# Hymba layer: sums of squares from the columns of x, with DVE additions and PE, and a new order of the first loads and index transposes

## The reference

```python
def rms_norm(x, g):
    xf = x.astype(jnp.float32)
    y = xf * lax.rsqrt(jnp.mean(xf * xf, axis=-1, keepdims=True) + EPS)
    return (y * g.astype(jnp.float32)).astype(x.dtype)

def reference(x, norm_gain, w_in, w_out, final_gain):
    B, S, _ = x.shape                       # 1, 512, 1024
    ...
        u = rms_norm(h, norm_gain[layer])   # DEPTH = 1
        z = jnp.einsum('bsd,de->bse', u, w_in[layer])
        (q_a, k_a, v_a, g_a, q_i, k_i, w_i, q_r, k_r, v_r, g_r) = jnp.split(z, split_points, axis=-1)
        ...
        y_a = dsa_attention(q_a, k_a, v_a, q_i, k_i, w_i, topk).reshape(B, S, ATT_WIDTH)
        y_a = y_a * jax.nn.silu(g_a)
        ...
        y_r = retention(q_r, k_r, v_r).reshape(B, S, RET_V_WIDTH)
        y_r = y_r * jax.nn.silu(g_r)
        mix = jnp.concatenate([y_a, y_r], axis=-1)
        h = h + jnp.einsum('bse,ed->bsd', mix, w_out[layer])
    return rms_norm(h, final_gain)
```

## Time and profile before

| | |
|---|---|
| Time, median of 3 runs | 295.29 us (295.18 to 295.79) |
| The profiled execution | 295.84 us, its span 293.7 us |
| Granted clock of PE, mean of the span | 0.989 |
| Busy: PE, DVE, ACT, POOL | 281.2, 201.4, 143.1, 68.6 us |
| Moved by DMA | 30.09 MB |

### The profile page before, as it was taken

The page is one execution under the profiler, slowest core; times in us unless marked ns, Lnnn a source line. Parts: engine busy times, 40 slices in busy tenths (PEclk is TensorE's granted clock), DMA queues, the critical chain, the costliest instruction groups (busy, mean ns, idle before and its releaser), DMA issues.

```text
span 293.7 us, 4386 instructions
## 1 busy us (share of the span) xinstructions
PE 281.2 (96%) x1504; PEld 240.7 (82%) x1504; DVE 201.4 (69%) x410; ACT 143.1 (49%) x305; POOL 68.6 (23%) x121
## 2 busy tenths in 40 slices
PE   5998999999999999997999999999999999999991
PEld 5996888888878888886888888788888988888891
DVE  1865799999999997759984863629646634854341
ACT  4766946333544533571666444564534662350231
POOL 1027322335200049990400203022010020000211
PEclk9799999999999999999999999999999999999998
DMA  7997520422332072040404220130210407311123
GB/s 227 405 342 280 169 76 0 143 73 74 98 116 75 0 208 78 2 143 1 135 11 143 72 73 0 33 112 7 77 63 0 137 8 230 129 36 36 74 86 128
DMA packets 15092, 30.09 MB, mean 102 GB/s; under 512 B 1376, under 2 KB 2912, under 8 KB 15072
## 3 DMA queue, kind: packets, MB, share of 16 engines
q1 hardware_dynamic: 14064, 28.71, 30.3%
q10 hardware_dynamic: 1008, 1.12, 1.1%
HBM read 27.73 MB, written 2.10 MB: 102 GB/s over the span
## 4 chain that ended last, share of the span: by engine, by line
PE 75%; DVE 12%; DMA 5%; issue 3%; POOL 2%; ACT 1%; ACTq 0%; SPq 0%; POOLq 0%; DVEq 0%
PE bank L417 19%; PE bank L419 18%; PE bank L418 18%; PE bank L467 6%; DVE keys L1035 3%; PE bank L481 3%; DVE top L1033 3%; DMA x_h<-in_x 3%; DVE w_lo L947 2%; DMA w_raw<-in_w_in 2%; PE bank L495 2%; PE bank L496 2%; DVE k_stack L996 1%; PE bank L505 1%; PE bank L526 1%
## 5 line engine op out<-in xcount | busy, mean ns | idle before, releaser
L417 PE MATMUL bank<-w_hi,xT_hi 128*128 128x512 f32 (+1 forms) x296 | 116.6, 394 | 0.3 <-ACT v_att L643 0.3
L419 PE MATMUL bank<-w_hi,xT_lo 128*128 128x512 f32 (+1 forms) x296 | 114.0, 385 | 0.0
L418 PE MATMUL bank<-w_lo,xT_hi 128*128 128x512 f32 (+1 forms) x296 | 113.8, 385 | 0.0
L419 PEld LDWEIGHTS bank<-w_hi,xT_lo 128*128 128x128 f32 x296 | 55.6, 188 | 11.4
L417 PEld LDWEIGHTS bank<-w_hi,xT_hi 128*128 128x128 f32 x296 | 55.7, 188 | 10.9 <-ACT v_att L643 0.6
L418 PEld LDWEIGHTS bank<-w_lo,xT_hi 128*128 128x128 f32 x296 | 55.8, 189 | 9.9
L947 DVE TENSOR_TENSOR w_lo<-w_raw,w_hi 128x1024 fp32r<-128x1024 f32 (+1 forms) x39 | 46.9, 1217 | 17.1 <-ACT w_hi L597 16.8
L597 ACT ACTIVATE w_hi<-w_raw 128x1024 fp32r<-128x1024 f32 (+1 forms) x39 | 39.7, 1029 | 7.9 <-DMA w_raw<-in_w_in 4.5
L712 ACT ACTIVATE work<-work,small 128x128 f32<-128x128 f32 (+3 forms) x32 | 17.7, 556 | 34.0 <-DVE small L1058 34.0
L882 POOL TENSOR_TENSOR th<-zt,tab 128x64 f32<-128x64 f32 (+1 forms) x24 | 14.5, 605 | 59.3 <-ACT zt L647 59.1
L1033 DVE MAX8 top<-keys 128x8 f32<-128x256 f32 (+2 forms) x48 | 26.9, 560 | 1.3
(11 more groups left out here) (122 smaller groups left out, 378.0 us busy)
## 6 DMA issues: line engine op xcount, KB each, us to landing
w_raw<-in_w_in SPq DMA_DIRECT2D x28, 512.0 KB, 3.8
w_raw<-in_w_out SPq DMA_DIRECT2D x8, 512.0 KB, 3.7
x_h<-in_x SPq DMA_DIRECT2D x4, 512.0 KB, 8.3
retT<-in_x SPq DMA_DIRECT2D x8, 256.0 KB, 3.6
mix<-in_x_cols SPq DMA_DIRECT2D x3, 512.0 KB, 7.8
out<-x_h SPq DMA_DIRECT2D x4, 320.0 KB, 2.5
w_raw<-in_w_in SPq DMA_DIRECT2D x3, 324.0 KB, 7.0
out<-x_h ACTq DMA_DIRECT2D x4, 192.0 KB, 2.7
```

The source lines that it names most:

```text
L417: pe.matmul(o, xh, hi[:, kk, c0:c0 + w], start=first, stop=False)
L418: pe.matmul(o, xh, lo[:, kk, c0:c0 + w], start=False, stop=False)
L419: mm = pe.matmul(o, xl, hi[:, kk, c0:c0 + w], start=False, stop=last)
```

## The change

- The host puts the norm gain as 8 columns ahead of x_cols. SP loads them with k tile 0 in one transfer (x_first, in the room of kz). The separate gain transfer is gone.
- SP issues, in this order: x_first, first half of the first weights, k tile 1, second half of the weights, then units 1 to 3. ACT issues none of them.
- The rows of x are not loaded (they are loaded for the residual later, as before). ACT squares the columns of each unit after its weight copy (two squares of 512 columns for unit 0, one of 1024 for the others). DVE adds them up, unit by unit after its low part, then adds both halves. PE sums over the partitions with four products with a column of ones, after the last products of row block 0. DVE reads them, scales and adds EPS, behind the splits of units 4 and 5. POOL does the power and the halving.
- One more matmul on zeros.
- The index transposes 0 and 1 stand behind q 3 of group 4, 2 and 3 behind q 1 of group 5; the logits of groups 5 to 7 behind q 3. ACT reads the projection ahead of the relus, and DVE's index_lo(2) and (3) move to slot 5.

New semaphores (sq_done, sq_added, ones_done, ssq_mm, ms_done) take the place of sq_even, sq_odd and rows_in; their declarations are left out here.

```diff
@@ -58,7 +58,8 @@
...
 ROUNDS = TOPK // 8
-WARM_UP = 8
+WARM_UP = 9
+GAIN = KT
@@ -104,14 +105,10 @@
...
-def x_columns(x):
-    return x[0].reshape(SEQ, KT, P).transpose(2, 1, 0).reshape(P, KT * SEQ)
-def gain_columns(norm_gain):
-    return norm_gain[0].reshape(KT, P).T
+def x_columns(x, norm_gain):
+    x = x[0].reshape(SEQ, KT, P).transpose(2, 1, 0).reshape(P, KT * SEQ)
+    return np.concatenate([norm_gain[0].reshape(KT, P).T, x], axis=1)
@@ -186,7 +183,7 @@
...
         x_h = sb("x_h", [P, MT, D_MODEL])
-        x_rows, h_out = x_h, x_h
+        h_out = x_h
         qT = sb("qT", [P, PAIRS, SEQ])
@@ -208,7 +205,13 @@
...
         mix = sb("mix", [P, MT, 2 * ATT_W])
-        xT_raw = mix[:, :, :].rearrange("p m c -> p (m c)").rearrange("p (k t) -> p k t", k=KT)
+        x_flat = mix[:, :, :].rearrange("p m c -> p (m c)")
+        x_first = kz[:, :, :].rearrange("p m c -> p (m c)")[:, 0:GAIN + SEQ]
+        def xT_raw(k):
+            return x_first[:, GAIN:] if k == 0 else x_flat[:, k * SEQ:(k + 1) * SEQ]
         th = sb("th", [P, CW])
@@ -219,9 +222,10 @@
...
         small = sb("small", [P, 128])
-        squares = [half.rearrange("p a c -> p (a c)") for half in (v_ret[:, 0:2, :], work[:, 0:2, :], v_ret[:, 2:4, :], work[:, 2:4, :])]
+        squares = [v_ret[:, 0:2, :], v_ret[:, 2:4, :], work[:, 0:2, :], work[:, 2:4, :]]
+        total = squares[0]
         idx_z = v_att[:, :, 0:IDX_ROW]
-        gain = small[:, 0:8]
+        gain = x_first[:, 0:GAIN]
         ssq, rstd, half_rstd = small[:, 8:12], small[:, 12:16], small[:, 16:20]
@@ -230,6 +234,7 @@
...
         minus_half, ms_eps = small[:, 84:88], small[:, 88:92]
+        ones = small[:, 104:105]
         x_again = retT[:, 0:4, :]
@@ -312,16 +317,14 @@
...
-            x_flat = mix[:, :, :].rearrange("p m c -> p (m c)")
-            sp.dma_start(x_flat[:, 0:SEQ], x_cols[:, 0:SEQ]).then_inc(x_in0, 16)
-            sp.dma_start(x_flat[:, SEQ:2 * SEQ], x_cols[:, SEQ:2 * SEQ]).then_inc(x_in1, 16)
+            sp.dma_start(x_first, x_cols[:, 0:GAIN + SEQ]).then_inc(x_in0, 16)
+            sp.dma_start(unit_half(w_raw, 0, 0), w_in[0, 0:P, BASE:BASE + IDX_W]).then_inc(w_first_in, 16)
+            sp.dma_start(x_flat[:, SEQ:2 * SEQ], x_cols[:, GAIN + SEQ:GAIN + 2 * SEQ]).then_inc(x_in1, 16)
+            sp.dma_start(unit_half(w_raw, 0, 1), w_in[0, P:2 * P, BASE:BASE + IDX_W]).then_inc(raw_in[0], 16)
             for u in range(1, QS):
-                part = slice(u * KQ * SEQ, (u + 1) * KQ * SEQ)
-                sp.dma_start(x_flat[:, part], x_cols[:, part]).then_inc(x_in[u], 16)
+                a, e = u * KQ * SEQ, (u + 1) * KQ * SEQ
+                sp.dma_start(x_flat[:, a:e], x_cols[:, GAIN + a:GAIN + e]).then_inc(x_in[u], 16)
                 load_unit(u)
-                if u >= 2:
-                    for m in (2 * u - 4, 2 * u - 3):
-                        sp.dma_start(x_rows[:, m, :], x[0, m * P:(m + 1) * P, :]).then_inc(rows_in[m], 16)
             sp.dma_start(tab[:, 0:TAB_EARLY], table[:, 0:TAB_EARLY]).then_inc(tab_early_in, 16)
@@ -383,6 +386,14 @@
...
                 mm.then_inc(proj_done, 1)
+            def sums_of_squares():
+                pe.wait_ge(ones_done, 1)
+                pe.wait_ge(sq_added, QS)
+                for m in range(MT):
+                    mm = pe.matmul(mid_ps[:, m:m + 1], total[:, 0, m * P:(m + 1) * P], ones, start=True, stop=True)
+                mm.then_inc(ssq_mm, 1)
@@ -546,15 +557,15 @@
...
                 last_products(QS - 1, m)
+                if m == 0:
+                    sums_of_squares()
...
                 proj(g, 1)
-                if g == MT:
-                    transpose_index(0)
-                    transpose_index(1)
-                if MT < g < 2 * MT:
-                    index_logits(g - MT)
+                if g == MT + 1:
+                    transpose_index(2)
+                    transpose_index(3)
                 if g >= RET0 + 1 and (g - RET0) % 2 == 1 and (g - RET0) // 2 < MT - 1:
@@ -564,8 +575,10 @@
...
                 if g == MT:
-                    transpose_index(2)
-                    transpose_index(3)
+                    transpose_index(0)
+                    transpose_index(1)
+                if MT < g < 2 * MT:
+                    index_logits(g - MT)
                 retention = RET0 <= g < RET0 + 2 * MT
@@ -597,20 +610,19 @@
...
             def x_hi(k):
-                act.activation(xT_hi[:, k, :], xT_raw[:, k, :], ACT.Copy, scale=gain[:, k:k + 1]).then_inc(xhi_done, 1)
-            def square_x(m):
-                act.wait_ge(rows_in[m], 16)
-                act.activation(squares[m], x_rows[:, m, :], ACT.Square, scale=D_MODEL ** -0.5,
-                               accum_out=ssq[:, m:m + 1]).then_inc(sq_even, 1)
-            act.dma_start(unit_half(w_raw, 0, 0), w_in[0, 0:P, BASE:BASE + IDX_W]).then_inc(w_first_in, 16)
-            act.dma_start(gain, gain_cols).then_inc(gain_in, 16)
-            act.dma_start(unit_half(w_raw, 0, 1), w_in[0, P:2 * P, BASE:BASE + IDX_W]).then_inc(raw_in[0], 16)
+                act.activation(xT_hi[:, k, :], xT_raw(k), ACT.Copy, scale=gain[:, k:k + 1]).then_inc(xhi_done, 1)
+            def square_x(u):
+                if u == 0:
+                    for k in range(KQ):
+                        act.activation(squares[0][:, k, :], xT_raw(k), ACT.Square).then_inc(sq_done, 1)
+                else:
+                    act.activation(squares[u], x_flat[:, u * KQ * SEQ:(u + 1) * KQ * SEQ].rearrange("p (k t) -> p k t", k=KQ),
+                                   ACT.Square).then_inc(sq_done, 1)
             act.wait_ge(ident_done, 1)
...
             act.activation(junk[:, 0:1], ident[:, 0:1], ACT.Exp).then_inc(warmed, 1)
-            act.wait_ge(gain_in, 16)
             act.wait_ge(x_in0, 16)
@@ -619,13 +631,13 @@
...
             act.activation(unit_half(w_hi, 0, 1), unit_half(w_raw, 0, 1), ACT.Copy).then_inc(whi_done, 1)
+            square_x(0)
             for u in range(1, QS):
...
                 split_hi(u)
-                if u >= 2:
-                    square_x(2 * u - 4)
+                square_x(u)
@@ -753,18 +765,18 @@
...
                     mix_hi(g - (GROUPS - 1))
+                if g == MT + 1:
+                    transposed_out(2)
+                    transposed_out(3)
+                if g >= MT + 2:
+                    transposed_out(g - 2)
+                if g < GROUPS:
+                    project_out(g)
                 if g == MT:
...
                     relus(g - MT)
-                if g >= MT + 2:
-                    transposed_out(g - 2)
-                if g < GROUPS:
-                    project_out(g)
-                if g == MT:
-                    transposed_out(2)
-                    transposed_out(3)
                 if 0 <= g - ATT0 - 1 < STEPS:
@@ -828,11 +840,12 @@
...
             pool.memset(minus_half, -0.5).then_inc(minus_half_done, 1)
+            pool.memset(ones, 1.0).then_inc(ones_done, 1)
             pool.wait_ge(minus_half_done, 1)
-            pool.wait_ge(sq_even, 2)
-            pool.wait_ge(sq_odd, 2)
-            rsqrt(rstd, ssq, ms_eps, rstd_done, 0)
+            pool.wait_ge(ms_done, 1)
+            pool.tensor_tensor(rstd, ms_eps, minus_half, ALU.pow).then_inc(rstd_done, 1)
+            pool.wait_ge(rstd_done, 1)
             pool.tensor_scalar(half_rstd, rstd, 0.5, None, ALU.mult).then_inc(hrstd_done, 1)
@@ -950,14 +963,9 @@
...
                 dve.wait_ge(xhi_done, k + 1)
-                dve.scalar_tensor_tensor(out=xT_lo[:, k, :], in0=xT_raw[:, k, :], scalar=gain[:, k:k + 1],
+                dve.scalar_tensor_tensor(out=xT_lo[:, k, :], in0=xT_raw(k), scalar=gain[:, k:k + 1],
                                          in1=xT_hi[:, k, :].bitcast(F32), op0=ALU.mult,
                                          op1=ALU.subtract).then_inc(xlo_done, 1)
-            def square_x(m):
-                dve.wait_ge(rows_in[m], 16)
-                dve.tensor_tensor_reduce(out=squares[m], in0=x_rows[:, m, :], in1=x_rows[:, m, :], scale=1.0 / D_MODEL,
-                                         scalar=0.0, op0=ALU.mult, op1=ALU.add, accum_out=ssq[:, m:m + 1]).then_inc(sq_odd, 1)
@@ -971,10 +979,16 @@
...
                 split_lo(u)
-                if u >= 2:
-                    square_x(2 * u - 3)
+                dve.wait_ge(sq_done, u + 2)
+                if u > 1:
+                    dve.wait_ge(sq_added, u - 1)
+                dve.tensor_tensor(total, total, squares[u], ALU.add).then_inc(sq_added, 1)
+            dve.wait_ge(sq_added, QS - 1)
+            dve.tensor_tensor(total[:, 0, :], total[:, 0, :], total[:, 1, :], ALU.add).then_inc(sq_added, 1)
             split_lo(QS)
             split_lo(QS + 1)
+            dve.wait_ge(ssq_mm, 1)
+            dve.tensor_scalar(ms_eps, mid_ps[:, 0:MT], 1.0 / D_MODEL, EPS, ALU.mult, ALU.add).then_inc(ms_done, 1)
             split_lo(QS + 2)
@@ -1174,8 +1188,11 @@
...
                 if g == MT:
```

(7 more changed lines are left out.)

13 lines of the change are left out of this document (6 added, 7 removed).

## The result

The changed kernel takes 298.12 us in the median (297.82 to 299.53, 5 runs) against 295.79 us before (295.18 to 296.76, 5 runs): a ratio of 1.0086, 95% interval 1.0056 to 1.0115. So it is slower by 2.3 us, where 1.2 were forecast. The profiled execution took 299.46 us, its span 297.5 us. The kernel before has such long executions too, 296.76 us here.

What follows compares the result with a forecast made beforehand. PE and DVE both nearly full from 42.4 to 86 us, DVE pacing. Minus 1.2 at the start and minus 1.1 at the gap are swallowed; scores(2) 1.2 late gives 295.29 + 1.2 = 296.5 us, range 294.3 to 298.2.

Steps and rivals of the forecast that it cites:

- First product: Start of PE: x_first lands at 4.2 us and products begin near 5.5 instead of 6.70, 1.2 us gained.
- Second half of the weights: First weights' second half, fourth on SP's queue: lands at 6.3 us, between 5.6 and at worst 8.4.
- The rival in which it lands at 8.4: Second half of first weights stays late, delaying squares 2 us and the chain behind: 298.5 us, chance 0.11.
- Landings up to unit 1: Unit 0's squares end at 8.0 us, unit 1's x tiles there by then: nothing in the sum, bound 0.5 late.
- Additions, sums, power: Norm chain: pair sum at 19.4, hidden ones products 0.84, power and halving done at 23.4; group 4 at 24.2, 0.9 later.
- Unit 7: With transposes moved away, PE waits 0.7 us for unit 7's low weights, out of the 1.11 us gap saved.
- Scores(2): Row block 2's index scores, held by logits behind q 3 of group 6: start at 45.4 instead of 44.14, 1.2 us late.
- DVE paces to T: Up to the transposes behind k_stack, 86.03 us before: DVE's 1.2 us lateness reaches PE as k_stack waits near 1 us.
- The loads as a whole: New transfer order at the start: booked as a 1.2 us gain, swallowed because DVE's later delay counts.
- Absorbed: Rival: unseen slack in the top-k chain absorbs DVE's delay, time within 0.2 us, 295.2; chance 0.13.
- PE paces: Rival: ACT and DVE keep up and PE's earlier, full-clock start counts: 293.3 us, half of it 294.3; chance 0.18.
- The half clock of the start: PE's slow clock after early idleness, 1.7 us: counts for the faster rival, nothing in the forecast, as DVE sets group 4.

Runs made afterwards that it cites:

- C1: Changed kernel with both halves of the first weights issued on ACT's queue again, gain still with k tile 0: 297.73 us, ratio 1.0047.
- B4: Kernel before with only the new loads (gain with k tile 0, first weights on SP's queue, nine warm-up matmuls): 297.45 us, ratio 1.0052.
- B1: Changed kernel without DVE's four additions, so only k tile 0's squares are summed: 298.51 us, ratio 1.0057.
- A1: Changed kernel with index transposes, logits, relus and index_lo back in their old places: 297.92 us, ratio 1.0080.
- A4: Kernel before with top-k rounds moved later (four a slot in slots 5 to 9, then two): 299.95 us, ratio 1.0129.
- C4: Kernel before with the gain in k tile 0's transfer and nine warm-up matmuls, first weights left on ACT's queue: 297.04 us, ratio 1.0041.
- B3: Changed kernel with DVE reading PE's sums between the splits of units 4 and 5: 298.15 us, ratio 1.0076.
- D2: C4 with the large table issued behind unit 8 on SP's queue: 296.40 us, ratio 1.0017.
- E1: Changed kernel in the old transpose and logits order, first weights on ACT's queue, table behind unit 8, ACT not waiting for the halving: 297.51 us, ratio 1.0058.
- D3: D2 with index transposes moved as in the change, logits(2) and (3) kept between q 1 and q 2: 300.36 us, ratio 1.0135.
- A2: Kernel before with only the new places of index transposes, logits and relus: 297.01 us, ratio 1.0046.
- D1: Kernel before with only the large table issued behind unit 8 instead of ahead of it: 295.53 us, ratio 0.9994.

## Why the prediction was right in sign and short in size

**The step that failed** is the landing of the first loads, which the sum put at nothing: "this counts nothing in the sum (bound: 0.5 late)". It measured 0.48 us at group 4. With 0.26 between the logits and scores(2), 0.24 from there to T, and 0.06 that the sum rounded away (45.4 less 44.14 is 1.26), the 1.2 us forecast become the 2.24 measured at T. The mechanism, a late DVE that PE meets at k_stack, held.

- **First product.** Forecast 5.5, it was 4.90. ACT's first copy started at 3.67 behind a wait of 1.45 us for the transfer, so x_first was there about 0.5 us before the forecast 4.2. The early start kept the clock: the granted clock was 1.00 from 8 to 11 us, 0.50 before. As forecast, nothing later gained by it: PE waited 0.44, 1.14 and 0.72 us for ACT and DVE instead.
- **Second half of the weights.** Forecast 6.3, copied at 6.98. The rival in which it lands at 8.4 had a time of 298.5, close to 298.12, but it isn't what happened. In C1, on ACT's queue and with the gain folded in, the half was there by 6.85; so it wasn't the move to SP's queue that brought it.
- **Landings up to unit 1: the term that failed.** ACT was to be done with unit 0's copies at 6.8 and its squares at 8.0, when the x tiles of unit 1 had to be there. It waited 1.22 us for k tile 1 (5.98), which the prediction gave no time of its own, and 0.28 for the second half of the weights (6.98), so the squares began at 7.36 and ended at 8.50; the x tiles of unit 1 then cost 0.15 more (8.65). All of it was still there at group 4, 24.68 instead of 24.2. C1 shows that 0.4 of this is the first weights on SP's queue. I had taken the rate of before for the new order, 327 GB/s where 165 came.
- **Additions, sums, power.** Pair sum done at 19.96 (19.4 forecast), so the step from the squares was right to 0.1. The ones' products took 1.02 us for the 0.84 of a far row, hidden as said. No collision at the halving (0.25), as said.
- **Unit 7.** Forecast a wait of 0.7, measured 0.43. Unit 8's load was waited for 0.85 us at 29.09; it cost nothing, as DVE waited for the transposes anyway.
- **Logits(2)** at 44.77, 20.09 us behind group 4; forecast 20.1. **Scores(2)** 21.46 behind it; forecast 21.2, the second small term: from the logits to the scores it took 1.37 us instead of 1.1. 1.26 + 0.48 + 0.26 are the measured 2.00. Scores(1) were late by the same 0.7 us: 39.12 for 38.4.
- **DVE paces to T.** Right: 2.00 at scores(2) became 2.24. The 0.24 more weren't forecast; 0.14 of them lies in the pair of splits ahead of scores(3), 2.40 us from start to start of the scores instead of 2.26, beside POOL's 1.24 and 1.30 us products. The waits for k_stack came to 1.6 us where I said near 1.
- **The loads as a whole: wrong in kind, and hidden in the sum.** I booked the new order of transfers as a gain of 1.2 us that is swallowed. By itself it is a loss (B4 1.18 at T, interval [1.0027, 1.0077]). I never asked what DVE waited for at 30.63 us, just ahead of the stretch that I had found to pace the kernel: the copy of unit 8, and that for its transfer. In the changed kernel this is partly healed, since the rows of x are gone, and partly hidden behind the moved transposes.
- **Absorbed, PE paces.** Neither: in B1 half of an earlier group 4 was waited away at k_stack in the profile, and in A1 a DVE in time met a PE that waited for POOL.
- **The half clock of the start** was worth nothing at group 4, as the forecast had it. A4 with the start of before kept 1.00 from 8 to 11 us, and its group 4 came at 23.19 behind a wait of 1.25 us, where the kernel before came at 23.31 behind 0.32.

Not settled: why gain and k tile 0 in one transfer delay units 7 and 8 by 0.9 us in C4, when the rows of x and group 4 move by 0.15. SP's issue of unit 8 took 0.37 us at 23.73 before, but 1.69 in C4 and 1.44 in A4, the two whose unit 8 is late behind an almost unmoved group 4 (C4, then A4):

```profile
23.93 1.69 SPq L316 DMA_DIRECT2D w_raw<-in_w_in  x1
```

```profile
23.63 1.44 SPq L313 DMA_DIRECT2D w_raw<-in_w_in  x1
```

As A4 has the start of before, the long issue doesn't need the new transfers. Whether they make it more frequent, and whether the sixteen engines or the queue's room holds it up, wasn't separated.

## What to carry to other kernels

When a view shows which engine paces a stretch, follow that engine's first instruction in the stretch back to what released it; a transfer there is a term of its own, and an edit that never touches it can still move it. Where two engines are both nearly full, a saving on either is only worth what the other has to spare, so undo and add each part singly and in pairs before believing a sum. Work that stands between two uses of late data is a cover; price the gap that opens when it moves.

## What the runs showed of the hardware

- **DVE and POOL.** A POOL operation that meets a DVE weight split is held for 0.8 to 1.0 us in the cases seen, whatever its size: 0.25 to 1.02 us (halving), 0.29 to 1.27 (copy), 0.35 to 1.34 (rotation), 1.03 to 1.87 (power). DVE's splits hardly lengthen (1.22 to 1.24, sometimes 1.39). The Trainium skill (SBUF — State Buffer, Who interferes with whom) calls the ports that the two share an exclusive lock; a delay that doesn't grow with POOL's own size agrees with that. This fell on the path in A1, B3, D2 and E1, and in the kernel before (the halving).
- **The clock.** In the changed kernel PE stood 1.68 us at 136.8 and got a granted clock of 0.78 and 0.70 behind it; the kernel before stood 1.72 us at 134.6 and kept 1.00. D3 fell to 0.55 behind 1.84 us of waiting, A1 kept 1.00 behind 2.12. In the start of before, the granted clock from 8 to 11 us was 0.50 behind a wait of 2.11, 0.51 in A2 (1.78) and 0.53 in D1 (1.67), but 1.00 in A4 (1.74). So the gap near 136 us is a risk of 1.6 us in a single execution, not a fixed price, and in these rows a wait's length alone doesn't tell.
- **Issue.** SP's issue takes 0.4 to 0.7 us each for the first eight transfers of the changed kernel, 1.15 for the ninth (at 4.72 us), and 1.74 for the large table at 21.54. That of unit 8 takes 0.37 before, 1.44 in A4 and 1.69 in C4. A load can so be late at its issue already.
